# Second pass of the final LayerNorm for tiles 0, 2 and 4: on VectorE, or as a product with a diagonal matrix on TensorE

## The reference

```python
def layer_norm(x, g, b):
    mu = jnp.mean(xf, axis=-1, keepdims=True)
    xc = xf - mu
    var = jnp.mean(xc * xc, axis=-1, keepdims=True)
    y = xc * lax.rsqrt(var + LN_EPS) * g + b
...
m = grouped_moe(x, w_router, b_router, w_up[l], w_down[l])
x = layer_norm(DEEPNORM_ALPHA * x + m, ln2_g[l], ln2_b[l])
```

## Time and profile before

| | us |
|---|---|
| median of 3 runs | 1670.3 |
| lowest and highest | 1667.24, 1670.33 |
| profiled execution | 1669.88 |
| its span | 1668.2 |
| VectorE busy in the span | 1176.0 |
| ScalarE busy | 845.4 |
| TensorE (matmul) busy | 1596.2 |
| GpSimd busy | 183.5 |

### The profile page before, as it was taken

One profiled execution on the slowest core, in us unless ns is written; L12 is line 12 of the kernel. 1 busy time (PEld: TensorE's weight loads), 2 busy tenths in 40 slices (PEclk: granted clock), 3 DMA queues, 4 the chain that ended last, 5 costly groups with the idle time before them and its releaser, 6 DMA issues.

```text
span 1668.2 us, 20247 instructions
## 1 busy us (share of the span) xinstructions
PE 1596.2 (96%) x7711; PEld 1321.9 (79%) x7711; DVE 1176.0 (70%) x1472; ACT 845.4 (51%) x1174; POOL 183.5 (11%) x219
## 2 busy tenths in 40 slices
PE   7999999999999999999999997999999999999981
PEld 6788888888888888888788885788888888888770
DVE  3755868495666666332575666799999999998884
ACT  3113121214556555325221333688888888887773
POOL 0000000202212220000000001111111111111120
PEclk9999999999999999999999997999999999999995
DMA  5144534645232331411553566899999999999966
GB/s 160 39 82 73 128 71 85 79 73 158 80 112 66 108 87 59 145 46 49 169 176 123 174 221 235 338 369 377 370 359 357 353 353 357 351 344 365 350 237 215
DMA packets 156985, 329.29 MB, mean 197 GB/s; under 512 B 15919, under 2 KB 85551, under 8 KB 156890
## 3 DMA queue, kind: packets, MB, share of 16 engines
q1 hardware_dynamic: 140746, 289.69, 53.8%
q0 software_dynamic: 16144, 38.32, 7.7%
HBM read 296.74 MB, written 48.52 MB: 207 GB/s over the span
## 4 chain that ended last, share of the span: by engine, by line
PE 88%; DMA 6%; DVE 3%; issue 1%; SPq 1%; ACT 1%; POOLq 0%; DVEq 0%; ACTq 0%
PE ps L753 53%; PE ps L1050 26%; DMA e_raw<-in_w_down 3%; PE ps L854 2%; PE ps L839 2%; PE ps L1057 1%; DMA e_raw<-in_w_up 1%; DVE e_lo L1868 1%; PE ps L998 1%; PE ps L1063 1%; DMA x_raw<-in_x 1%; DVE zout L1928 1%; DVE zout L1921 1%; PE ps L986 0%; SPq L547 0%
## 5 line engine op out<-in xcount | busy, mean ns | idle before, releaser
L1868 DVE TENSOR_TENSOR e_lo<-e_raw,e_hi 128x1024 fp32r<-128x1024 f32 x376 | 436.2, 1221 | 24.4 <-ACT e_hi L1364 20.8
L1364 ACT ACTIVATE e_hi<-e_raw 128x1024 fp32r<-128x1024 f32 x376 | 367.8, 1050 | 25.3 <-DMA e_raw<-in_w_down 17.9
L753 PE MATMUL ps<-xt_hi,w_hi 128*128 128x512 f32 x896 | 303.3, 395 | 2.4 <-DVE xt_lo L1467 2.4
L753 PE MATMUL ps<-xt_lo,w_hi 128*128 128x512 f32 x896 | 299.0, 390 | 0.0
L753 PE MATMUL ps<-xt_hi,w_lo 128*128 128x512 f32 x896 | 298.8, 390 | 0.0
L753 PEld LDWEIGHTS ps<-xt_hi,w_lo 128*128 128x128 f32 x896 | 168.4, 188 | 35.9
L753 PEld LDWEIGHTS ps<-xt_hi,w_hi 128*128 128x128 f32 x896 | 168.3, 189 | 35.2 <-DVE xt_lo L1467 2.6
L753 PEld LDWEIGHTS ps<-xt_lo,w_hi 128*128 128x128 f32 x896 | 168.8, 188 | 33.0
L1500 DVE TENSOR_TENSOR w_lo<-w_raw,w_hi 128x512 fp32r<-128x512 f32 x136 | 94.9, 703 | 130.8 <-ACT w_hi L1133 127.4
L1133 ACT ACTIVATE w_hi<-w_raw 128x512 fp32r<-128x512 f32 x136 | 83.7, 628 | 202.1 <-PE ps L753 199.6
L1050 PE MATMUL ps<-e_hi,xe_hi 128*128 128x512 f32 x512 | 164.4, 402 | 8.5 <-DVE e_lo L1868 7.9
(11 more groups left out here) (280 smaller groups left out, 2254.7 us busy)
## 6 DMA issues: line engine op xcount, KB each, us to landing
e_raw<-in_w_up SPq DMA_DIRECT2D x128, 1024.0 KB, 21.9
e_raw<-in_w_down SPq DMA_DIRECT2D x64, 1024.0 KB, 21.7
w_raw<-in_w_in SPq DMA_DIRECT2D x64, 256.0 KB, 4.9
w_raw<-in_w_gate SPq DMA_DIRECT2D x48, 256.0 KB, 3.5
gates_d<-gate_t POOLq DMA_DIRECT2D x16, 512.0 KB, 3.4
gate_s<-gates_d SPq DMA_DIRECT2D x16, 512.0 KB, 3.6
qkv_d<-qkv POOLq DMA_DIRECT2D x12, 512.0 KB, 3.8
w_raw<-in_w_branch SPq DMA_DIRECT2D x24, 256.0 KB, 3.7
```

The costliest lines, as they stand in the source:

```text
L753: last = nc.tensor.matmul(o(h, c1 - c0), st(k), mv(k, c0, c1), start=start and k == nk[0] and n == 0, stop=h in stop and k == nk[-1] and n ...
L1364: nc.scalar.activation(e_hi[:, (UPT + s) % RSPL, :], e_raw[r][:, s % 2, :], ACT.Copy).then_inc(e_h, 1)
L1868: nc.vector.tensor_tensor(e_lo[:, sp_, :], e_raw[raw_slot(b, s)][:, s % 2, :], e_hi[:, sp_, :], ALU.subtract).then_inc(e_all, 1)
```

## The change

The second pass of tiles 0, 2 and 4 leaves VectorE. For each of them ScalarE scales the 128x128 identity by the column of reciprocals (`diagonal`), which gives a diagonal matrix in SBUF. TensorE multiplies the first pass's result by it, after a product of one row of ones with the one row of `ln2_b` has put the bias into the same PSUM banks; the 1024 columns are two halves, so four products per tile, all fp32. ScalarE copies the two banks to `zout` (`take_z`), and that copy releases the store. Tiles 0 and 4 use the banks 4 and 5, tile 2 the banks 6 and 7, so tile 4 waits for the copy of tile 0. The other five tiles are done as before. SyncE stores in the order 1, 3, 0, 5, 2, 6, 7, 4.

```diff
@@ -74,6 +74,8 @@
 RRAW = len(RING_KB)
 STATIC = NE - 1
 O_PIECE = 8
+ON_PE = (0, 2, 4)
+STORES = (1, 3, 0, 5, 2, 6, 7, 4)
 ALPHA = 2.0 ** 0.25
 EPS = 1e-5
...
@@ -263,6 +265,7 @@
         zout = at("zout", [P, TT, D], FP32, 144)
         zsq = at("zsq", [P, D], FP32, 176)
         zst = at("zst", [P, TT, 16], FP32, 180)
+        z_rstd = [at(f"z_rstd{i}", [P, P], FP32, 184 + i / 2) for i in range(len(ON_PE))]
...
+        z_diag, z_mm = sem("z_diag"), sem("z_mm")
...
+
+        def recips(t):
+
+            return 3 + 2 * t
+
+        def z_bank(t):
+
+            return 4 + 2 * (ON_PE.index(t) % 2)
...
@@ -562,9 +574,12 @@
             sp.wait_ge(ye_out, 16 * (last_b + 1))
             for t in range(TT):
                 sp.dma_start(zin[:, t, :], z_d[t * P:(t + 1) * P, :]).then_inc(tile_in[t], 16)
-            for t in range(TT):
-                sp.wait_ge(out_ok, t + 1)
-                sp.dma_start(out[0, t * P:(t + 1) * P, :], zout[:, t, :]).then_inc(out_dma[t % 4], 16)
+            for i, t in enumerate(STORES):
+                if t in ON_PE:
+                    sp.wait_ge(evac[0], 1 + CT * len(KINDS) // 2 + ON_PE.index(t) + 1)
+                else:
+                    sp.wait_ge(out_ok, t + 1 - sum(u < t for u in ON_PE))
+                sp.dma_start(out[0, t * P:(t + 1) * P, :], zout[:, t, :]).then_inc(out_dma[i % 4], 16)
             for u in range(4):
                 sp.wait_ge(out_dma[u], 16 * TT // 4)
@@ -1103,6 +1118,18 @@
             pe.wait_ge(ht_l, last_b + 1)
             for s in range(DNT):
                 weights(item(last_b + 1, s), UPT + s, (ht_hi, ht_lo), s, 0, DNT)
+
+            for i, t in enumerate(ON_PE):
+                pe.wait_ge(z_diag, i + 1)
+                if i >= 2:
+                    pe.wait_ge(evac[0], 1 + CT * len(KINDS) // 2 + i - 1)
+                if i == 0:
+                    pe.wait_ge(par9_in, 32)
+                for h in range(2):
+                    o = ps[:, z_bank(t) + h, :]
+                    nc.tensor.matmul(o, ones_e[0:1, 0:1].to_broadcast([1, P]), lnb2[0:1, h * HALF:(h + 1) * HALF], start=True, stop=False)
+                    last = nc.tensor.matmul(o, z_rstd[i][:], zout[:, t, h * HALF:(h + 1) * HALF], start=False, stop=True)
+                last.then_inc(z_mm, 1)
...
 
-            for t in range(TT):
+            def deviation(t):
                 st = zst[:, t, :]
                 act.wait_ge(tile_in[t], 32)
                 nc.scalar.activation(st[:, 1:2], zin[:, t, D:D + 1], ACT.Copy, scale=-1.0 / D).then_inc(z_mean, 1)
@@ -1429,6 +1456,28 @@
                 act.wait_ge(z_var, t + 1)
                 nc.scalar.activation(st[:, 3:4], st[:, 2:3], ACT.Sqrt, scale=1.0 / D, bias=eps[:]).then_inc(std9, 1)
 
+            def diagonal(t):
+                act.wait_ge(ln9, recips(t))
+                nc.scalar.activation(z_rstd[ON_PE.index(t)][:], ident[:], ACT.Copy, scale=zst[:, t, 4:5]).then_inc(z_diag, 1)
+
+            def take_z(t):
+                act.wait_ge(z_mm, ON_PE.index(t) + 1)
+                nc.scalar.activation(zout[:, t, :], flat(z_bank(t)), ACT.Copy).then_inc(evac[0], 1)
+
+            deviation(0)
+            deviation(1)
+            diagonal(0)
+            deviation(2)
+            deviation(3)
+            diagonal(2)
+            deviation(4)
+            deviation(5)
+            diagonal(4)
+            take_z(0)
+            deviation(6)
+            deviation(7)
+            take_z(2)
+            take_z(4)
@@ -1915,17 +1964,26 @@
             split_h(last_b)
 
             dve.wait_ge(par9_in, 32)
-            for t in range(TT + 1):
-                if t < TT:
-                    dve.wait_ge(z_mean, t + 1)
-                    nc.vector.scalar_tensor_tensor(zout[:, t, :], zin[:, t, 0:D], zst[:, t, 1:2], lng2[:], ALU.add, ALU.mult).then_inc(ln9, 1)
-                if t == 0:
-                    continue
-                st, z = zst[:, t - 1, :], zout[:, t - 1, :]
-                dve.wait_ge(std9, t)
-                nc.vector.reciprocal(st[:, 4:5], st[:, 3:4]).then_inc(ln9, 1)
-                dve.wait_ge(ln9, 2 * t + (t < TT))
-                nc.vector.scalar_tensor_tensor(z, z, st[:, 4:5], lnb2[:], ALU.mult, ALU.add).then_inc(out_ok, 1)
+            done = Chain(ln9)
+
+            def first_pass(t):
+                dve.wait_ge(z_mean, t + 1)
+                done.go(nc.vector.scalar_tensor_tensor(zout[:, t, :], zin[:, t, 0:D], zst[:, t, 1:2], lng2[:], ALU.add, ALU.mult))
+
+            def second_pass(t):
+                dve.wait_ge(std9, t + 1)
+                done.go(nc.vector.reciprocal(zst[:, t, 4:5], zst[:, t, 3:4]))
+                if t in ON_PE:
+                    assert done.n == recips(t)
+                    return
+                done.join()
+                nc.vector.scalar_tensor_tensor(zout[:, t, :], zout[:, t, :], zst[:, t, 4:5], lnb2[:], ALU.mult, ALU.add).then_inc(out_ok, 1)
+
+            first_pass(0)
+            for t in range(1, TT):
+                first_pass(t)
+                second_pass(t - 1)
+            second_pass(TT - 1)
```

## The result

| | before | after |
|---|---|---|
| median of 6 runs, us | 1669.62 | 1677.03 |
| lowest and highest | 1667.24, 1670.33 | 1674.18, 1678.34 |
| span of the profiled execution | 1668.2 | 1675.6 |
| first load of `z_d` issued at | 1640.02 | 1639.89 |
| from there to the end of the span | 28.18 | 35.71 |

The changed kernel is slower: ratio 1.0044, 95% interval 1.0033 to 1.0055. All of it lies in the last stage. Both kernels issue the first load of `z_d` at the same time, within 0.13 us, and then the changed one needs 7.5 us more.

What follows compares the result with a forecast made beforehand. VectorE's back-to-back passes were taken to bound the final stage: -3.72 (passes removed) + 2.77 (idle waiting for ScalarE) + 1.25 (one more queued store) = +0.3 us with rounding, span 1668.5, median about 1670.6; range 1667.0 to 1674.3.

Steps and rivals of the forecast that it cites:

- Forecast gaps: Final stage: VectorE idles 0.63, 0.60 and 1.54 us before first passes of tiles 2, 4 and 6, waiting for ScalarE's means.
- Diagonals: ScalarE, final stage: each 128x128 scaling of the identity by a column of reciprocals takes 0.38 us.
- VectorE's end: Final stage: VectorE saves 3.72 us of passes, gives back 2.77 in idle, and ends 0.95 us earlier.
- the queue of stores: End of the kernel: the last stores' data queue in the DMA engines; one more store behind VectorE's last costs 1.25 us.
- the forecast's sum: Whole change: -3.72 + 2.77 + 1.25 = +0.3 us with rounding, span 1668.5; chance 0.60.
- TensorE costs nothing here: Final stage: TensorE ends tile 4 near 1660.9, before ScalarE wants it at 1661.57, so it adds no time.
- 8 x 0.855 = 6.84 us a tile: TensorE, final stage: time of a tile's four fp32 products at 1.2 GHz, from L1083's spacing; 3.44 at 2.4 GHz.
- the rows give no discount: TensorE's bias products: a one-row product costs what a full one does, 297 ns against 293 at 32 columns.
- Rival A: Final stage: TensorE's clock stays at 1.2 GHz, span ends 1672.2, 4.0 us slower, median 1674.3; chance 0.15.
- with either, tile 0 is done by 1652.9 to 1653.8: TensorE, final stage: with the clock back after 4.1 or 6.0 us, tile 0's products end then, tile 2's by 1656.3 to 1657.3.
- Both starts: Earlier low-clock TensorE work, at 1030.75 (L1083) and near 15.1, where the clock rose 4.1 and 6.0 us later.
- Against it: L1083's fp32 products did bring it back: Argument against the clock staying at 1.2 GHz: L1083's products began at 1030.75 and the clock rose near 1034.9.

Runs made afterwards that it cites:

- v1: e2 with ScalarE's list reordered, each diagonal one tile later and tile 0's copy behind tile 6's root; median 1667.69 us, ratio 0.9990 to the kernel before.
- e2: Changed kernel with the bias through the 128x128 identity and all 128 rows of ln2_b instead of one row; median 1668.48 us, ratio 0.9998 to before.
- e7: e2 with the store of tile 4 issued ahead of that of tile 7; one run, 1669.05 us, stage 28.71.
- e3: Changed kernel with 18 unread fp32 products of 512 columns on TensorE right behind the last expert; median 1673.42 us, ratio 1.0029 to before.
- e5: Changed kernel with each tile's two one-row products first, then its two diagonal ones; median 1669.86 us, ratio 1.0015 to before.
- e4: Kernel before plus 12 unread fp32 products of 512 columns over 128 rows, from the third tile's mean on; one run, 1667.73 us.
- e6: Kernel before plus 12 unread one-row fp32 products of 512 columns, from the third tile's mean on; one run, 1667.72 us.
- e12: Kernel before plus 12 unread fp32 products of 512 columns over 64 rows, from the third tile's mean on; one run, 1667.30 us.
- e8: Kernel before plus 12 unread pairs, a full 512-column product and a one-row 32-column one, from the third tile's mean on; one run, 1679.52 us.
- e10: Changed kernel with the bias product over 64 rows of ones and ln2_b instead of one; median 1675.87 us, ratio 1.0041 to before.
- e9: Kernel before plus 6 unread one-row products of 512 columns, then 10 full ones, from the third tile's mean on; one run, 1670.74 us.
- e11: Kernel before plus 12 unread pairs, a 512-column and a 32-column product, both over 128 rows, from the third tile's mean on; one run, 1669.62 us.

## Why the prediction was wrong

**Right: VectorE and ScalarE.** Forecast gaps 0.63, 0.60 and 1.54; measured 0.63, 0.56 and 1.47. Diagonals were forecast at 0.38 and took 0.39 to 0.40, copies 1.03 against 1.01 to 1.02. VectorE's end came 0.99 us earlier, counted from the first load (24.05 against 25.04), where 0.95 was forecast. v1 shows that the cause was the order of ScalarE's list: with it changed, the three gaps are 0.34 in all.

**Right: the queue of stores.** e2 is the kernel that the forecast's sum describes, with the clock up in time. Its stage is 28.93, 0.75 above before, where the sum gave +0.3; VectorE ended 0.2 later than the forecast (24.31 after the first load, 24.09 forecast), and from its last end to the span's end there are 4.6 us, 4.4 forecast. e7 shows that bytes set that end.

**Wrong: "TensorE costs nothing here".** Two steps of the working failed.

The first is the spacing, "8 x 0.855 = 6.84 us a tile". It was read from L1083, where every product has the same 128 rows of weights. Products with a different number of rows on either side start 0.29 to 0.30 us later at the low clock and 0.19 at the high one (2.00 against 1.70, 1.05 against 0.86 in e3 and e2). e5 has half of the changes and half of the cost; e4 and e6, 128 rows or one row throughout, have none. For 12 products that is 3.5 us. The sentence "the rows give no discount" for a one-row product was right, but it looked at the duration of one and not at the start of the next. It was read from L996, which has such changes on both sides, and the kernel before holds a hint of the cost there: L996's two records start at 921.62 and the first of L998 at 921.96, 0.34 us for two where the 16 of L998 behind them take 0.11 each. Rival A, with its 4.0 us for the clock, lacks these 3.5: 4.0 + 3.5 = 7.5, which is the growth of the stage from 28.18 to 35.71.

The second is the clock, "with either, tile 0 is done by 1652.9 to 1653.8". Both starts that it rests on were work over 128 rows. Rival A named the right doubt ("nothing in the trace shows how such a stretch affects the clock") and had a chance of 0.15. The runs put in its place: work over one row (e6) or 64 rows (e12) leaves the clock at 1.2 GHz for all of its 20.8 us; so does full-height work in which every second product has fewer rows (31 us in e8, 24 us in e10); full-height work with products of 512 columns, without a break, brings it up 3.4 to 5.7 us after its start (e2, e4, e7, e9, v1, and e11 with short ones in between). The changed kernel has both features, one-row products and a change at every product. Changes at every product were enough in e8, which has hardly any time in one-row products. One-row products were shown to be enough only where nothing else runs: in e5 they are half of the products, as in the changed kernel, and the clock rose in the profiled run. What it is about the changes that does it stays open. The argument "Against it: L1083's fp32 products did bring it back" transferred a row to work of another shape. The kernel before holds a warning against that, right ahead of L1083 (timeline, then a window):

```profile
1020.14 5.36 PE L1013 MATMUL ps<-vals,by_rank 128*128 128x64 f32 x24
```

```profile
1022.00:1024.00 2.00, 2.00 (x11) 2.00 (x11) 1.76 (x10) 0.00 (x0) 0.00 (x0) 0.50 0.85 147
```

From 1016.71 to 1025.50 TensorE runs full-height fp32 products of 32 columns (L998) and 64 columns (L1013) without a break, and the granted clock stays at 0.50 for these 8.8 us. So an unbroken stretch over 128 rows does not always bring the clock up either. Its products are short, and the number of columns belongs to what must be compared.

The Trainium skill ("TensorE: Matmul & The Clock Gate", Why this matters for your kernels) advises to keep TensorE busy continuously to get the full clock. Here the trace disagrees with it as a sufficient rule: 24 us without a break stayed at 0.50 in the changed kernel. The same page of the Trainium skill (Part 2) says that the weight load is pulled ahead of running matmuls when row groups do not conflict or the background buffer is its target; the 1.50 us of idle behind two joined loads, against 0.52 behind single ones in the earlier trace rows, fits loads that are not pulled ahead where the number of rows changes. Apart from the first product after an idle stretch, they stand joined in e5 just at the changes and singly in between, and in e2, where the weights change but not the rows, singly throughout. The runs show the gap; that the loader is its cause is a reading of them.

## What to carry to other kernels

A spacing or a clock read from one kind of matmul holds for that kind: before it is carried over, compare the number of rows of weights and of columns, of the product and of its neighbours. Where a bias or a sum goes through TensorE, a full-height product (identity by the broadcast row) takes no longer than a one-row product; between full-height ones it came here without the 0.3 us at each change, and the clock rose. And work handed from a full engine to a half-full one helps only if its place in the other's list does not make the first engine wait; moving four instructions here made the stage 2.0 us shorter (28.93 to 26.89).

## What the runs showed of the hardware that was not expected

- fp32 products of 512 columns over 1 or 64 rows, 20.8 us without a gap: granted clock 0.50 throughout (e6, e12). The same over 128 rows: up after 5.7 us (e4), in the other runs with full-height products of 512 columns without a break after 3.4 to 5.4 us (v1, e7, e9, e2, e11).
- Full-height fp32 products of 32 and 64 columns, 8.8 us without a break: 0.50 throughout (kernel before, 1016.71 to 1025.50).
- A change between products of different numbers of rows: 0.29 to 0.30 us at the low clock, 0.19 at the high one, per change; none between two different full-height weights (e2).
- Under such alternation a high clock fell after 7.3 us (e3).
- A short full-height product between long ones lets the clock rise after 5.4 us, though the pair takes 2.16 us (e11); a short one-row product keeps it at 0.50 for 31 us (e8).
